# Nine experts' weights cast to bf16 ahead instead of seven, three result row buffers instead of two, casts held until the next pass's tokens have landed, and the first expert's slots loaded alone

## The reference

```
gl = t @ w_group + b_group ; g_idx = argmax(gl)             # 1 of 4 groups
el = (t @ w_expert + b_expert)[group g_idx]                 # 4 experts of the group
top_v, top_i = lax.top_k(el, 2)                             # the 2 best of them
wts = softmax(top_v) * softmax(gl)[g_idx]
a = silu(t @ w1[e]) * (t @ w3[e])                           # w1, w3: 1024 x 256, for each of 16 experts
y = sum over the two experts e of wts * (a @ w2[e])         # w2: 256 x 1024
```

## Time and profile before

| what | value |
|---|---|
| time, median of 3 runs (lowest to highest) | 936.15 us (935.47 to 938.74) |
| the profiled execution: time, span of its slowest core (core 1) | 935.5 us, 934.0 us |
| spans of the 8 cores | 917.8 to 934.0 us |
| busy: PE, DVE, ACT, POOL | 741.8, 449.2, 343.6, 159.7 us |
| stage 1 and the wide convolution | to about 303 us |
| stage 3 with the router of the last pass | to about 635 us |
| experts | to about 855 us |
| gather, combine, final norm, output | to 934.0 us |

### The profile page before, as it was taken

One profiled execution on the slowest core, in us unless ns is written; L12 is line 12 of the kernel. 1 busy time (PEld: TensorE's weight loads), 2 busy tenths in 40 slices (PEclk: granted clock), 3 DMA queues, 4 the chain that ended last, 5 costly groups with the idle time before them and its releaser, 6 DMA issues.

```text
span 934.0 us, 15237 instructions; the slowest of 8 cores (917.8 to 934.0 us)
## 1 busy us (share of the span) xinstructions
PE 741.8 (79%) x4982; PEld 413.9 (44%) x4982; DVE 449.2 (48%) x1085; ACT 343.6 (37%) x568; POOL 159.7 (17%) x215
## 2 busy tenths in 40 slices
PE   0479999999987798998999988240999699993652
PEld 0235555566543353553544546120555355551541
DVE  1214324356646645655564446440455355551586
ACT  1435554433558043452361543320222122231331
POOL 4200001010000010220320321202244133332000
PEclk9779999999999899999999999675899999998775
DMA  9999999998324759289379697528699888993955
GB/s 181 209 216 193 240 228 296 205 200 136 61 46 115 148 174 110 67 212 107 121 182 109 193 170 117 147 41 179 154 205 209 263 266 278 287 319 110 279 198 211
DMA packets 64308, 167.73 MB, mean 180 GB/s; under 512 B 15792, under 2 KB 28976, under 8 KB 60896
## 3 DMA queue, kind: packets, MB, share of 16 engines
q0 software_dynamic: 25536, 69.57, 44.1%
q1 hardware_dynamic: 38688, 97.12, 34.0%
HBM read 165.10 MB, written 66.04 MB: 247 GB/s over the span
## 4 chain that ended last, share of the span: by engine, by line
PE 59%; DVE 15%; DMA 11%; issue 7%; ACT 3%; another core or an unknown queue 1%; SPq 1%; POOL 1%; DVEq 1%; POOLq 0%; ACTq 0%
PE ps_all L487 20%; PE ps_all L982 6%; PE ps_all L1156 5%; DMA w1b<-w_in 5%; PE ps_all L1141 4%; PE ps_all L1143 4%; PE ps_all L816 4%; DMA yrows<-yrow,sid 3%; PE ps_all L674 3%; PE ps_all L961 2%; PE ps_all L967 2%; DVE xb L783 2%; PE ps_all L1130 1%; DMA xsb<-xslots 1%; DVE x2b L1247 1%
## 5 line engine op out<-in xcount | busy, mean ns | idle before, releaser
L487 PE MATMUL ps_all<-hT,w1b 128*128 128x448 bf16 (+1 forms) x800 | 151.8, 349 | 12.9 <-DMA w1b<-w_in 11.0
L487 PE MATMUL ps_all<-hT,wg 128*128 128x448 bf16 (+1 forms) x640 | 122.9, 348 | 0.0
L487 PEld LDWEIGHTS ps_all<-hT,w1b 128*128 128x128 bf16 x800 | 78.2, 99 | 78.8 <-issue 20.4
L1166 POOL DMA_INDIRECT yrows<-yrow,sid x64 | 64.5, 1007 | 146.3 <-DVE hE L1133 124.6
L487 PEld LDWEIGHTS ps_all<-hT,wg 128*128 128x128 bf16 x640 | 62.6, 99 | 52.1 <-issue 2.0
L1156 PE MATMUL ps_all<-wC,aT 128*104 128x512 bf16 x256 | 65.9, 388 | 11.4 <-ACT yrow L1161 7.8
L955 ACT ACTIVATE sig<-ps_all 128x448 bf16<-128x448 f32 (+1 forms) x64 | 32.3, 512 | 115.2 <-PE ps_all L487 105.9
L927 POOL DMA_INDIRECT xslots<-hrow,six x38 | 36.3, 954 | 201.5 <-DVE hrow L926 83.1
L1161 ACT ACTIVATE yrow<-ps_all 104x512 bf16<-104x512 f32 x64 | 38.2, 597 | 78.6 <-PE ps_all L1156 49.8
L982 PE MATMUL ps_all<-merged,wo 128*128 128x448 bf16 (+1 forms) x320 | 61.1, 352 | 6.5 <-DVE merged L974 5.0
L1164 DVE CAST yrow<-ps_all 104x512 bf16<-104x512 f32 x64 | 43.9, 689 | 24.7 <-ACT yrow L1161 17.7
(11 more groups left out here) (220 smaller groups left out, 1148.8 us busy)
## 6 DMA issues: line engine op xcount, KB each, us to landing
xslots<-ft SPq DMA_DIRECT2D x4, 3432.0 KB, 45.2
xsb<-xslots SPq DMA_DIRECT2D x16, 858.0 KB
ring<-w_ada POOLq DMA_DIRECT2D x24, 512.0 KB, 17.0
wpre<-w POOLq DMA_DIRECT2D x21, 512.0 KB, 29.7
gat<-yrows SPq DMA_DIRECT2D x36, 224.0 KB, 9.8
xs<-xT SPq DMA_DIRECT2D x4, 1792.0 KB, 16.1
xb<-xT SPq DMA_DIRECT2D x4, 1792.0 KB, 10.0
x2s<-xb SPq DMA_DIRECT2D x8, 896.0 KB, 3.8
```

Of the source, the lines that this page charges most:

```text
L487: S.add(PE, lambda e: [e.matmul(PS(bank, P.n), wt[:, kc, j * 128:(j + 1) * 128], h_[:, kc, :], start=(kc == 0), stop=(kc == NDC - 1)) for ...
L1166: S.add(POOL, lambda e, t=t: [e.indirect_dma_start(out=ys_d[:, :], out_offset=bass.IndirectOffsetOnAxis(ap=sid[0:TP, ex, t:t + 1], axis=0) ...
```

## The change

- `EPRE` goes from 9 to 7: experts 7 to 15 are cast ahead, nine instead of seven. The casts of two experts follow each of the passes 0 to 3, and that of expert 15 pass 4. Two experts fewer, 7 and 8, are loaded by casting DMAs on GpSimd during stage 4, and two more by SyncE.
- The casts and expert loads after passes 0 to 3 no longer name the pass's DRAM stores as what they read, but the first block of the tile `xb` into which the next pass's tokens are being loaded (`nxt_x`).
- `yrow` has three buffers, the third at an offset that the stages before have left and the gather uses later.
- The load of the second expert's slots names the first slot tile as read, so that it waits for the first load; the load of expert 4's weights comes after it in the code and names the second slot tile.

```diff
-    wp_d = nc.dram_tensor("wpre", [7, 128, 6144], BF16).ap()
+    wp_d = nc.dram_tensor("wpre", [9, 128, 6144], BF16).ap()
...
-        yrow = [al("yrow%d" % i, [TP, 4, 1024], BF16, off=aE + 13312 + 8192 * i, unit=1024) for i in range(2)]
+        yrow = [al("yrow%d" % i, [TP, 4, 1024], BF16, off=o_, unit=1024) for i, o_ in enumerate((aE + 13312, aE + 21504, aD + 20992))]
...
-        EPRE = 9
+        EPRE = 7
...
+        def nxt_x(P):
+            return [("xb%d" % (P.idx % 2), 0)] if P.idx < 4 else [("x2d", 4, 0), ("x2d", 4, 1)]
+
...
             if P.idx == 2:
-                load_expert(0, [("x2d", 2, 0), ("x2d", 2, 1)])
+                load_expert(0, nxt_x(P))
             if P.idx == 3:
-                load_expert(1, [("x2d", 3, 0), ("x2d", 3, 1)])
+                load_expert(1, nxt_x(P))
                 load_expert(2)
-            for ex in {0: (9, 10), 1: (11, 12), 2: (13, 14), 3: (15,)}.get(P.idx, ()):
-                precast(ex, [("x2d", P.idx, 0), ("x2d", P.idx, 1)])
+            for ex in {0: (7, 8), 1: (9, 10), 2: (11, 12), 3: (13, 14), 4: (15,)}.get(P.idx, ()):
+                precast(ex, nxt_x(P))
...
         run_all(n2["rows"])
-        load_expert(4)
         run_all(n2["weights"])
...
-        def ex_load(ex):
+        def ex_load(ex, after=()):
             b = ex % 3
             S.add(SP, lambda e: [e.dma_start(out=xsb[b][:], in_=xs_d[ex * CAP:(ex + 1) * CAP, :].rearrange("(p t) d -> p t d", t=4))],
-                  reads=allxs, writes=[("xsb%d" % b, t) for t in range(4)], dma=("xsl", b), ndma=1, name="ld_xs")
+                  reads=allxs + list(after), writes=[("xsb%d" % b, t) for t in range(4)], dma=("xsl", b), ndma=1, name="ld_xs")
...
         def ex_Y(ex, ts=range(4)):
-            b, slot = ex % 2, ex % NWS
+            b, slot, yb_ = ex % 2, ex % NWS, ex % 3
...
         ex_load(0)
-        ex_load(1)
+        ex_load(1, [("xsb0", 0)])
+        load_expert(4, [("xsb1", 0)])
         ex_load(2)
```

More of the change, by code:

```diff
@@ L1158, in ex_Y @@
                           reads=["wC%d" % slot, ("aT%d" % b, 0), ("aT%d" % b, 1)], writes=[("ps", bank)], name="y_mm")
-                    o = yrow[b][:, t, h * 512:(h + 1) * 512]
+                    o = yrow[yb_][:, t, h * 512:(h + 1) * 512]
                     if h == 0:
                         S.add(ACT, lambda e, o=o, bank=bank: [e.activation(out=o, in_=ps_all[0:TP, bank, :], func=AF.Copy)],
-                              reads=[("ps", bank)], writes=[("yrow%d" % b, t)], name="y_ev")
+                              reads=[("ps", bank)], writes=[("yrow%d" % yb_, t)], name="y_ev")
                     else:
                         S.add(DVE, lambda e, o=o, bank=bank: [e.tensor_copy(o, ps_all[0:TP, bank, :])],
-                              reads=[("ps", bank)], writes=[("yrow%d" % b, t)], name="y_ev2")
+                              reads=[("ps", bank)], writes=[("yrow%d" % yb_, t)], name="y_ev2")
                 S.add(POOL, lambda e, t=t: [e.indirect_dma_start(
                     out=ys_d[:, :], out_offset=bass.IndirectOffsetOnAxis(ap=sid[0:TP, ex, t:t + 1], axis=0),
-                    in_=yrow[b][:, t, :], in_offset=None, bounds_check=bound["t"], oob_is_err=False)],
-                    reads=["sid%d" % ex, ("yrow%d" % b, t)], writes=[("ys", ex, t)], dma=("yst", b, t), ndma=1, name="y_scatter")
+                    in_=yrow[yb_][:, t, :], in_offset=None, bounds_check=bound["t"], oob_is_err=False)],
+                    reads=["sid%d" % ex, ("yrow%d" % yb_, t)], writes=[("ys", ex, t)], dma=("yst", yb_, t), ndma=1, name="y_scatter")
         def mk_dgw(gt):
```

## The result

The changed kernel took 932.57 us (median of 20 runs), the kernel before 939.09 us beside it on the same chips. The ratio is 0.9929 (95% interval 0.9901 to 0.9958): faster by 0.7%, some 6.6 us. In some executions, whatever the kernel, the cores of one die run slower; all ratios, and the medians and means of the experiments, leave these out, and where a profile caught one (own key; own key with late token loads), the other four cores are read. Forecast were 922 us, and 14 us of gain.

The account below looks back on a forecast made before the run. Mostly TensorE at work, with late result scatters and the first slot load as removable waits. Profiled 935.5 - 11.7 (yrow stalls) - 7.9 (slot load) + 6.2 (L985 wait) = 922.1, predicted 922 us; range 914 to 931.

Parts of the forecast that it names:

- Edit 4: Casts name the next pass's tile as read: in pass 4 the first L985 waits for them, costing 6.2 us (0.9 to 17.5).
- "remote" stall: VectorE's 6.36 us stall in pass 4 on core 1, with no release in the trace; assumed covered by the new wait.
- The landing: Pass 4: the twelve DMAs land at 593.5, from 577.4 plus 13.2 for three more casts and 2.9 for the later start.
- The core: Loss at L985 taken as core 1's 6.2 us; up to 12 on cores like 7, which enter the experts 7 us earlier.
- edit 3: First slot load alone, before the experts: 5.5 us instead of 13.38, a gain of 7.9 us (0.9 to 9.6).
- Edits 1 and 2: Expert stage: nine experts cast ahead and three row buffers remove the yrow stalls, a gain of 11.7 us (0 to 11.7).
- Rival C: Part of two gains stays away: slot load still 9 us, or a yrow stall of some 4 us; 926, chance 0.10.
- A: Rival: in pass 4 the casts land early, at 588.2, so L985 hardly waits, loss 0.9; 916.8 us, chance 0.15.
- B: Rival: the "remote" stall isn't covered but comes again behind the new wait in pass 4; 928.5 us, chance 0.15.
- D: Rival: pass 4's twelve DMAs take some 6.5 us each, loss 39.9 at L985; 955.8 us, chance 0.04.

Follow-up runs that it names:

- own key: Changed kernel, but the casts wait for the token load through a key of their own that nothing writes later: 921.57 us, ratio 0.9835.
- own key with late token loads: Changed kernel with that separate key, and the x2b loads issued behind experts 13 and 14 instead of 9 to 13: 918.65 us, ratio 0.9822.
- stores: Changed kernel, but the casts wait for the pass's DRAM stores as before the change: 919.40 us, ratio 0.9812.

## Why the prediction was wrong

**Edit 4 was the step that failed, by its size.** The mechanism was right in every part: L985 of pass 4 released by a `wpre` DMA, 0.94 us a block behind it, no second "remote" stall. (In pass 3, where I had no wait, core 1 had one of 3.9 us, and its next token load was issued 1.6 us later.) Two things were too small.
- The landing. Forecast 577.4 + 13.2 + 2.9 = 593.5 on core 1; measured 577.4 + 15.4 + 4.6 = 597.4. A cast beside the gates of pass 4 took 5.1 us, over the 4.4 that I took and the 3.6 to 4.96 that I had read. And the shift of the start wasn't the start-up of one DMA. I had argued that token load and casts move the same bytes side by side or in turn; but the group starts 8.7 us later and only half of that comes back.
- The core. I put the loss of core 1 in the sum, where a "remote" stall of 6.36 us was going to be covered. The four cores without that stall lost 12.8 us on the mean, those with it 6.6. I had said so, up to 12, and then let them off because they stood some 7 us earlier; but which four cores have the stall changes from execution to execution, so the core that is last in one execution isn't in the next. The mean loss was 9.7 us, and doing without the key gave back 7.5 (own key) and 9.1 (stores).

With 9.7 for 6.2 the forecast would have been 925.6. The sum promised 13.4 us, and the mean span of the two profiles fell by 6.9. Of the missing 6.5, 3.5 are this step; 1.1 are edit 3 with the path around it, 0.8 the turns, and 1.1 the last stage, which I had as unchanged. The median is 10.6 us over the forecast and not 6.5 for another reason too: the kernel before took 939.09 beside it, 2.9 more than the 936.15 from which I had started, and that has nothing to do with the change. The same kernel repeated on another chip took 927.77, inside my range of 914 to 931; that the range was missed is partly such chance, that the gain falls well short isn't (0.9929 and 0.9906, against a forecast of 0.985).

**Edit 3** was right in kind, 5.7 on the mean core (6.3 on core 1) for 7.9: the load alone takes 6.9 us, and I had taken 5.5.

**Edits 1 and 2** gave 10.9 on the mean core for 11.7. No wait at `yrow` is left, as said. Missed was what is late next in that stage: the last slot loads, behind added weight loads and token loads. Rival C had the shared DMA engines, at `yrow`; they showed at `xsb`, on core 3 above all, whose turns gained 5.3. Core 1 has no wait at `xsb` behind the first, and gained 9.4 instead of 11.7; what took the 2.3 isn't settled. And I had counted two edits for one stall where either nearly suffices.

**The chances.** A (casts early) is out: the group landed late, not early. B's time, 928.5, is nearest but its mechanism, a second "remote" stall, didn't come. D's pace of 6.5 us a cast wasn't reached. C's place was next to right. The measured 932.57 lies 1.6 us over the range: the true loss at L985 was inside its bounds (0.9 to 17.5), but the upper end of these bounds had been given no chance of its own.

## What to carry to other kernels

A key that is named only to delay a DMA also blocks the next writer of that key until the DMA has landed. If only the delay is wanted, use a key that nobody else writes. When several edits serve one stall, price the stall once, and ask which transfers used the pause that it gave. And take a loss that differs by core at its mean, not at the core that was last in one execution.

## Not expected of the hardware

- Casts from DRAM to DRAM (1 MB float32 to 512 KB bf16) took 5.1 us each in the group after pass 3 on core 1. The Trainium skill, page "DMA: Bandwidth & Descriptors", section "Anatomy of one DMA", gives 2.0 us plus the bytes at 436 GB/s for one DMA: an estimate of 4.4 us for the 1 MB read alone, and of 2.4 for each further one if the fixed part overlaps, as the prediction had it. The measured time is over both.
- The "remote" stall at L985 stands on four cores of one die at a time, cores 0 to 3 in some executions and 4 to 7 in others, at the same place of the program. In pass 4 of the changed kernel, with L985 waiting 12 us and more, none was seen in either of its two profiles; in pass 3 of the first, cores 0 and 1 had one of 6.0 and 4.2 us. Nothing in the trace names its cause, and no run here tried it.
